# A kernel of two transformer blocks: the FFN row factor moves from its input to Silu and product, three last down units go by token tile, and the next stage's first rows are turned in the last unit

## What is computed

```python
def rmsnorm(x, g):
    y = xf * lax.rsqrt(jnp.mean(xf * xf, axis=-1, keepdims=True) + EPS)
    return y.astype(x.dtype) * g

def swiglu(x, w_gate, w_up, w_down):
    return (jax.nn.silu(x @ w_gate) * (x @ w_up)) @ w_down

h = h + 0.5 * rmsnorm(swiglu(rmsnorm(h, ffn1_pre_g), gate, up, down), ffn1_post_g)   # FFN1
h = h + rmsnorm(merged @ w_out, mix_post_g)                                          # mixer's output
h = h + 0.5 * rmsnorm(swiglu(rmsnorm(h, ffn2_pre_g), ...), ffn2_post_g)              # FFN2
x = x + y @ w_out_2                                                                  # second block's output
x = x + swiglu(rmsnorm(x, ffn_norm_g_2), ...)                                        # FFN3
```

## Time and profile before

| | |
|---|---|
| median of 3 runs | 1169.39 us (1167.99 to 1169.9) |
| profiled execution | 1170.61 us |
| its span | 1168.8 us |
| TensorE busy | 1123.3 us (96%) |
| TensorE weight loads | 942.0 us (81%) |
| VectorE busy | 694.4 us (59%) |
| ScalarE busy | 586.1 us (50%) |
| mean granted TensorE clock | 0.990 of full speed |

### The profile page before, as it was taken

The page is one execution under the profiler, slowest core; times in us unless marked ns, Lnnn a source line. Parts: engine busy times, 40 slices in busy tenths (PEclk is TensorE's granted clock), DMA queues, the critical chain, the costliest instruction groups (busy, mean ns, idle before and its releaser), DMA issues. The chain is left out here.

```text
span 1168.8 us, 13926 instructions
## 1 busy us (share of the span) xinstructions
PE 1123.3 (96%) x5748; PEld 942.0 (81%) x5748; DVE 694.4 (59%) x793; ACT 586.1 (50%) x828; POOL 21.4 (2%) x35
## 2 busy tenths in 40 slices
PE   5999999999999999999999999999899999999997
PEld 4888887899989986777778888877778877888886
DVE  4644554676767777776666445446665656555443
ACT  4543434554567765664455434345566535343333
POOL 0000000000001110000000000000000000000000
PEclk9999999899999999999999999999999999999999
DMA  9656653655566544445456565554633345566550
GB/s 306 213 180 189 195 193 115 218 179 180 176 188 199 185 154 167 143 123 184 146 185 210 183 195 195 183 152 140 203 109 126 131 139 182 181 191 197 187 180 36
DMA packets 132206, 202.74 MB, mean 173 GB/s; under 512 B 5760, under 2 KB 98816, under 8 KB 131888
## 3 DMA queue, kind: packets, MB, share of 16 engines
q1 hardware_dynamic: 129328, 190.68, 50.6%
q0 software_dynamic: 2816, 11.18, 2.8%
HBM read 200.76 MB, written 1.08 MB: 173 GB/s over the span
## 5 line engine op out<-in xcount | busy, mean ns | idle before, releaser
L913 DVE TENSOR_TENSOR WL<-RAW,WH 128x2048 fp32r<-128x2048 f32 (+1 forms) x181 | 406.2, 2265 | 111.1 <-ACT WH L437 111.1
L437 ACT ACTIVATE WH<-RAW 128x2048 fp32r<-128x2048 f32 (+1 forms) x181 | 338.5, 1888 | 12.6 <-DMA RAW<-in_w_out 3.7
L1479 PE MATMUL PS<-WH,XTH 128*128 128x512 f32 (+1 forms) x676 | 267.3, 395 | 0.0
L1481 PE MATMUL PS<-WH,XTL 128*128 128x512 f32 (+1 forms) x676 | 263.4, 390 | 0.0
L1480 PE MATMUL PS<-WL,XTH 128*128 128x512 f32 (+1 forms) x676 | 262.8, 389 | 0.0
L1479 PE MATMUL ACC<-WH,KTH 128*128 128x512 f32 (+1 forms) x476 | 188.7, 396 | 5.7 <-DVE WL L913 3.5
L1481 PE MATMUL ACC<-WH,KTL 128*128 128x512 f32 (+1 forms) x476 | 185.8, 390 | 0.0
L1480 PE MATMUL ACC<-WL,KTH 128*128 128x512 f32 (+1 forms) x476 | 185.4, 390 | 0.0
L1481 PEld LDWEIGHTS PS<-WH,XTL 128*128 128x128 f32 x676 | 126.8, 188 | 26.5
L1479 PEld LDWEIGHTS PS<-WH,XTH 128*128 128x128 f32 x676 | 127.0, 188 | 24.9 <-issue 0.5
L1480 PEld LDWEIGHTS PS<-WL,XTH 128*128 128x128 f32 x676 | 127.1, 188 | 24.6
(11 more groups left out here) (264 smaller groups left out, 1283.0 us busy)
## 6 DMA issues: line engine op xcount, KB each, us to landing
RAW<-in_w_in SPq DMA_DIRECT2D x50, 1024.0 KB, 5.2
RAW<-in_ffn_w_gate SPq DMA_DIRECT2D x44, 512.0 KB, 4.0
RAW<-in_ffn_w_up SPq DMA_DIRECT2D x44, 512.0 KB, 5.0
RAW<-in_ffn_w_down SPq DMA_DIRECT2D x22, 1024.0 KB, 4.9
RAW<-in_w_gate SPq DMA_DIRECT2D x22, 512.0 KB, 4.0
RAW<-in_w_up SPq DMA_DIRECT2D x22, 512.0 KB, 5.0
RAW<-in_w_down SPq DMA_DIRECT2D x11, 1024.0 KB, 4.9
RAW<-in_ssd_w_branch SPq DMA_DIRECT2D x8, 1024.0 KB, 5.0
```

The costliest lines, as they stand in the source:

```text
L437: nc.scalar.activation(WH[:, s, 0:n], RAW[:, s, 0:n], ACT.Copy).then_inc(w_hi, 1)
L913: tt(WL[:, s, 0:n], RAW[:, s, 0:n], WH[:, s, 0:n].bitcast(F32), ALU.subtract).then_inc(w_lo, 1)
L1479: mm(ps, stat_hi, mov_hi, start=first, stop=False)
L1481: return mm(ps, stat_lo, mov_hi, start=False, stop=last)
```

## The change

1. The input of an FFN (n = 0, 2, 4) is XN = H * gain, without the row factor. The factor comes in behind the product: as the scale of Silu and as a scalar of the product for HS. So XN waits for H alone, and the Silus wait for the factor. The squares for these factors write to a scratch JUNK, no longer to XN. ScalarE computes them after the copy XTH of tile 0 (n = 2, 4) or of both tiles (n = 0).
2. The last three down units of an FFN go by token tile: 8, 9, 10 for tile 0, then for tile 1, the turn of the last hidden rows behind unit 8 of tile 0. Those last hidden rows go to LASTH and LASTL, places in XTH and XTL, since KTH and KTL still hold the two steps before. In step 10 two weight splits move from behind the Silus to in front of them.
3. The next stage's tile 0 is turned (`first_tile`) inside the last unit: before the last 6 matmuls of FFN1 and FFN2, and before the last 12 of the second block's output product. For n = 2 it stays behind the last unit.

The core of the diff:

```diff
+        JUNK = SCR[:, 0:1024]
+        LASTH, LASTL = (x[:, 0:4, P:2 * P] for x in (XTH, XTL))
...
+                junk = JUNK if n in (0, 2, 4) else XN[:, t, :]
+                own.link(nc.scalar.activation(junk, H[:, t, :], ACT.Square, accum_out=SS[:, t:t + 1]))
...
-                    if 0 < j < FF_STEPS - 1:
+                    if j:
                         split_hi()
                         split_hi()
                     c = u0 + FF_AT["a", j]
                     for t in range(NT):
                         chunk_tile(c, c + 1, t)
-                        nc.scalar.activation(SG[:, t, :], PS[4 + t][:, 0:256], ACT.Silu).then_inc(gate_ok, 1)
+                        act.wait_ge(rstd_ok, 4 * f + t + 1)
+                        nc.scalar.activation(SG[:, t, :], PS[4 + t][:, 0:256], ACT.Silu,
+                                             scale=RS[:, t:t + 1]).then_inc(gate_ok, 1)
                     if 1 <= j < FF_STEPS - 2:
                         split_hi()
-                    if j in (0, FF_STEPS - 1):
+                    if j == 0:
                         split_hi()
                         split_hi()
...
+                if m in (1, 3):
+                    if m == 1:
+                        y_rstd(m, unit, 0, half)
+                        y_rstd(m, unit, 1, half)
+                    xn_hi(m + 1, 0)
+                    h_rstd(m + 1, 0)
+                    h_rstd(m + 1, 1)
+                    nc.scalar.preload_act_table(next_table)
+                    xn_hi(m + 1, 1)
+                    split_hi()
+                    return
...
             ln_exp()
-            h_rstd(0, 0)
             xn_hi(0, 0)
             split_hi()
+            split_hi()
+            xn_hi(0, 1)
+            h_rstd(0, 0)
             h_rstd(0, 1)
-            split_hi()
             nc.scalar.preload_act_table(ACT.Silu)
-            xn_hi(0, 1)
             split_hi()
             ffn(0, U_FFN1)
...
             def xn(n, t):
-                dve.wait_ge(rstd_ok, NT * n + t + 1)
+                if n in (1, 3):
+                    dve.wait_ge(rstd_ok, NT * n + t + 1)
+                elif n == 0:
+                    dve.wait_ge(x_loaded[t], 16)
+                else:
+                    dve.wait_ge(h_done, NT * (n - 1) + t + 1)
                 dve.wait_ge(gpre_loaded, 16 * (n + 1))
                 for q in range(2):
                     a = slice(q * 512, (q + 1) * 512)
-                    stt(XN[:, t, a], H[:, t, a], RS[:, t:t + 1], GPRE[:, a], ALU.mult, ALU.mult).then_inc(xn_ok, 1)
+                    if n in (1, 3):
+                        ins = stt(XN[:, t, a], H[:, t, a], RS[:, t:t + 1], GPRE[:, a], ALU.mult, ALU.mult)
+                    else:
+                        ins = tt(XN[:, t, a], H[:, t, a], GPRE[:, a], ALU.mult)
+                    ins.then_inc(xn_ok, 1)
...
-                        tt(HS[:, t, :], PS[4 + t][:, 256:512], SG[:, t, :], ALU.mult).then_inc(h_ready, 1)
+                        stt(HS[:, t, :], PS[4 + t][:, 256:512], RS[:, t:t + 1], SG[:, t, :], ALU.mult,
+                            ALU.mult).then_inc(h_ready, 1)
...
+            def first_tile(n):
+                turn_normed(n, 0, 0)
+                turn_normed(n, 0, 1)
...
-                down(FF_STEPS - 3)
-                turn_hidden(FF_STEPS - 1)
-                pe.wait_ge(hT_lo, n0 + FF_STEPS - 1)
-                pe.wait_ge(w_lo, u0 + FF_AT["d", FF_STEPS - 2] + 1)
-                s = FF_STEPS - 2
+                s = FF_STEPS - 3
                 for t in range(NT):
-                    for n in range(2):
+                    for n in range(3):
                         c = u0 + FF_AT["d", s + n]
+                        if t == 0 and n == 1:
+                            turn_hidden(FF_STEPS - 1)
                         pe.wait_ge(w_lo, c + 1)
                         pe.wait_ge(hT_lo, n0 + s + n + 1)
-                        ins = rows_part(c, [(0, t), (1, t)], False, n == 1, half=(s + n) % 2)
+                        half_at = 2 if n == 2 else (s + n) % 2
+                        rows_part(c, [(0, t)], False, n == 2, half=half_at)
+                        if t and n == 2 and then:
+                            then()
+                        ins = rows_part(c, [(1, t)], False, n == 2, half=half_at)
...
+            first_tile(0)
             norm(0, U_FFN1)
-            ffn(0, U_FFN1)
+            ffn(0, U_FFN1, then=lambda: first_tile(1))
             norm(1, U_XZ)
...
+            first_tile(2)
             norm(2, U_FFN2)
-            ffn(1, U_FFN2)
+            ffn(1, U_FFN2, then=lambda: first_tile(3))
...
-            by_pairs(20, U_OUT2, BUF2, ready=lambda s: pe.wait_ge(merged, 4 + (1, 3, 2, 4)[s]), turned=True)
+            by_pairs(20, U_OUT2, BUF2, ready=lambda s: pe.wait_ge(merged, 4 + (1, 3, 2, 4)[s]), turned=True, then=lambda: first_tile(4))
             norm(4, U_FFN3)
             ffn(2, U_FFN3)
```

More of the change, by code:

```diff
@@ L456, in h_rstd @@
                 own.wait() if own.n else None
-                own.link(nc.scalar.activation(XN[:, t, :], H[:, t, :], ACT.Square, accum_out=SS[:, t:t + 1]))
+                junk = JUNK if n in (0, 2, 4) else XN[:, t, :]
+                own.link(nc.scalar.activation(junk, H[:, t, :], ACT.Square, accum_out=SS[:, t:t + 1]))
                 own.link(nc.scalar.activation(RS[:, t:t + 1], SS[:, t:t + 1], ACT.Ln, scale=1.0 / D, bias=EPS))
@@ L476, in hidden_hi @@
                     act.wait_ge(h_turned, n0 + j + 1)
-                    nc.scalar.activation(KTH[:, half_of(j)], PS[6][:], ACT.Copy).then_inc(hT_hi, 1)
+                    if j == FF_STEPS - 1:
+                        nc.scalar.activation(LASTH, PS[6][:].rearrange("p (k c) -> p k c", k=4), ACT.Copy).then_inc(hT_hi, 1)
+                    else:
+                        nc.scalar.activation(KTH[:, half_of(j)], PS[6][:], ACT.Copy).then_inc(hT_hi, 1)
                 for j in range(FF_STEPS):
@@ L517, in boundary @@
                     return
-                if m in post_no:
-                    y_rstd(m, unit, 1, half)
+                y_rstd(m, unit, 1, half)
                 xn_hi(m + 1, 0)
                 h_rstd(m + 1, 1)
-                if next_table:
-                    nc.scalar.preload_act_table(next_table)
                 xn_hi(m + 1, 1)
@@ L934, in hidden_lo @@
                     dve.wait_ge(hT_hi, n0 + j + 1)
-                    tt(KTL[:, half_of(j)], PS[6][:], KTH[:, half_of(j)].bitcast(F32), ALU.subtract).then_inc(hT_lo, 1)
+                    if j == FF_STEPS - 1:
+                        tt(LASTL, PS[6][:].rearrange("p (k c) -> p k c", k=4), LASTH.bitcast(F32),
+                           ALU.subtract).then_inc(hT_lo, 1)
+                    else:
+                        tt(KTL[:, half_of(j)], PS[6][:], KTH[:, half_of(j)].bitcast(F32), ALU.subtract).then_inc(hT_lo, 1)
                 for j in range(FF_STEPS):
@@ L1408, in _, with turn_normed @@
             mm = nc.tensor.matmul
-            def norm(n, c):
-                def turn(t, q):
-                    pe.wait_ge(xn_ok, 4 * n + 2 * t + q + 1)
-                    if t:
-                        pe.wait_ge(xt_lo, 4 * n + q + 1)
-                    for k in range(4):
-                        j = 4 * q + k
-                        ins = nc.tensor.transpose(PS[6 + q][:, k * P:(k + 1) * P], XN[:, t, j * P:(j + 1) * P], IDENT)
-                    ins.then_inc(xn_turned, 1)
-                turn(0, 0)
-                turn(0, 1)
+            def turn_normed(n, t, q):
+                pe.wait_ge(xn_ok, 4 * n + 2 * t + q + 1)
+                if t:
+                    pe.wait_ge(xt_lo, 4 * n + q + 1)
+                for k in range(4):
+                    j = 4 * q + k
+                    ins = nc.tensor.transpose(PS[6 + q][:, k * P:(k + 1) * P], XN[:, t, j * P:(j + 1) * P], IDENT)
+                ins.then_inc(xn_turned, 1)
+            def first_tile(n):
+                turn_normed(n, 0, 0)
+                turn_normed(n, 0, 1)
+            def norm(n, c):
                 pe.wait_ge(w_lo, c + 1)
@@ L1433, in norm @@
                 half(c + 1, 1, 0, 4, (0, 1))
-                turn(1, 0)
+                turn_normed(n, 1, 0)
                 half(c + 1, 1, 0, 4, (2, 3)).then_inc(chunk_half, 1)
-                turn(1, 1)
+                turn_normed(n, 1, 1)
                 pe.wait_ge(xt_lo, 4 * n + 3)
@@ L1509, in rows_part @@
                     a = slice(half * 512 + k * TOK + t * P, half * 512 + k * TOK + (t + 1) * P)
+                    hi, lo = (LASTH[:, 2 * k + t], LASTL[:, 2 * k + t]) if half == 2 else (KTH[:, a], KTL[:, a])
                     for h in range(2):
                         ws = slice(k * D + h * 512, k * D + (h + 1) * 512)
-                        ins = parts(PS[banks + 2 * t + h][:], KTH[:, a], KTL[:, a], WH[:, s, ws], WL[:, s, ws],
+                        ins = parts(PS[banks + 2 * t + h][:], hi, lo, WH[:, s, ws], WL[:, s, ws],
                                     first and k == 0, last and k == 1)
```

(2 more changed lines are left out.)

2 lines of the change are left out of this document (1 added, 1 removed).

## The result

The changed kernel takes **1176.47 us** in the median of 5 runs (1173.48 to 1178.73). The kernel before, timed between those runs, takes 1169.40 (5 runs). The ratio is 1.0058 with a 95% interval of 1.0038 to 1.0078, so the change costs between 4.4 and 9.1 us. The forecast was 1174.4 in a range of 1172.0 to 1178.0: the sign and the range hold, and the forecast's +5.0 lies in the measured interval, in its lower part.

A forecast was written before the change was run, and what follows sets the result against it. TensorE, busy nearly all the span, bounds the kernel; only added work or its waits count. 4.5 + 1.3 - 0.9 - 0.8 + 0.9 = +5.0 us on the median 1169.39 gives 1174.4, range 1172.0 to 1178.0.

The forecast's parts named there:

- Start, +4.5: Start of FFN1: factors and table load ahead of unit 2's split delay TensorE's step 1 by 4.5 us.
- Clock at the start, +1.3: Behind the start's wait: a certain fall to the lower clock, priced 0.5 to 2.3 us, value 1.3.
- FFN ends, -0.9: FFN1 and FFN2 ends: hidden-row wait goes, but squares still precede the copy; 0.45 us gained per joint, -0.9 together.
- Mixer's joint, -0.8: Joint after the mixer's output product: squares no longer held by the factor, first matmul at 599.7 against 600.33; -0.8 us.
- Second block's joint, +0.9: Joint after second block's output product: turn inside the unit waits 1.6 us for the late add; +0.9 us.
- The rule on transposes: Second block's joint: transposes don't count as busy for the clock gate, so it may lose 1.6 us more.
- Small edits, 0: Three-operand HS products, Silu scales from a row and a later freed unit: 0, or 0.1 us in step 1.
- The clock at the other joints: Joints other than the start: six stretches without a 128x512 matmul before and after, so 0 us, 1.6 each for the range.
- The first: Rival: two more joints fall to 1.2 GHz, or one and a longer start stretch; 1177.6 us, chance 0.20.
- The second: Rival: start's delay mostly hidden, or joints give their whole idle; 1168.6 to 1171.0 us, chance 0.10.
- third: Rival: ScalarE's order doesn't end these waits, so unit 2 and XTH copies aren't late; 1164.5 us, chance 0.04.

The follow-up runs named there:

- e1: Changed kernel with both row factors and the Silu table load put back before the tile 1 copies at the start; 1171.23 us, ratio 1.0015.
- e8: Changed kernel with 18 matmuls that nothing reads in TensorE's wait at the start, ahead of step 1 of FFN1; 1174.88 us, ratio 1.0050.
- e2: Changed kernel with XTH copied before the squares of tile 1's sum and XTL before VectorE's gain at the two FFN joints; 1174.38 us, ratio 1.0031.
- e3: Changed kernel with FFN3's first tile turned behind the second block's output product, not inside its last unit; 1174.88 us, ratio 1.0040.
- e4: Changed kernel with the next stage's first tile turned behind the last down unit of FFN1 and FFN2, not inside it; 1173.47 us, ratio 1.0035.
- e7b: Changed kernel with the start's order put back and nine matmuls that nothing reads in the wait at both FFN joints; 1168.77 us, ratio 0.9995.
- e5: Kernel before with only the three last down units by token tile, with their hidden copies and split order; 1169.19 us, ratio 0.9998.
- e6: Changed kernel with the start's order and all three first-tile turns put back, keeping the missing factor and down units by tile; 1166.42 us, ratio 0.9966.
- e12: Kernel before with only the down units by token tile, run again for a second profile; profiled execution 1165.21 us.
- e9: Kernel before with the three last down units by tile, plus five matmuls that nothing reads at both FFN joints; 1168.67 us, ratio 0.9984.

## Why the prediction was right, step by step

- **Start, +4.5.** Right. Unit 2 was split at 29.97 (forecast 29.6; the first matmuls ran longer at the lower clock in this execution, and the two factors began at 25.53 instead of 25.11), and TensorE waited 4.46 us. e1 takes the step away and gets 0.43 points of 0.58 back.
- **Clock at the start, +1.3.** Right in mechanism, as e8 shows, and too small in size: 1.6 in the changed kernel's trace, but 2.4 in those of e2, e3 and e4, above the 2.3 that I had as its upper end. I had priced one slow stretch of the usual length with a part of it inside the wait. In the changed kernel's trace it began only with the matmuls, so nothing was hidden; in the other three it did begin in the wait, but was twice as long (3.4 us lost by the windows, 2.4 of it in matmuls).
- **FFN ends, -0.9.** Right in mechanism and size. The KTL wait is gone, the two turns came in (0.93 where I had 0.87), the copy stayed behind the squares. The account gives -0.5 for FFN2 (-0.21 and -0.28); FFN1's can't be separated from the start within a few tenths. e4 and e2 show the two halves of the reason: the turn inside the unit costs 0.93 and gains nothing, and what ends the joint is the chain of tile 1.
- **Mixer's joint, -0.8.** Right: last matmul to first 2.64 instead of 3.40. The table's other 1.3 is the missing slow stretch.
- **Second block's joint, +0.9.** Right to a tenth in the chain: from the add's start to the turn 2.12 us (forecast 2.1), to the first matmul 5.98 (forecast 5.9), to the low matmuls 8.12 (forecast 8.1); the account has +2.65 - 1.82 = +0.8. The true wait was 1.31, not 1.6. Here the term held two effects of opposite sign that the prediction didn't part: e3 shows some 1.5 us lost by the turn's place against 0.7 won by the missing factor.
- **The rule on transposes.** No slow stretch followed this joint in the profiled run: the matmuls from 977.73 on stand 0.23 apart. Nor did one in e1, e2, e4, e7b and e8, which turn in the output unit too. The Trainium skill (TensorE: Matmul & The Clock Gate, Part 4: PE-mode transpose) says that transposes don't count as busy for the clock gate in the way matmuls do. Six traces without a fall speak rather against taking this stretch for idle as a whole, but they don't refute the page: waits with no transpose in them had no fall behind them either in many executions, as the 1.88 at 581 and the 2.25 at both FFN joints of this same trace.
- **Small edits, 0.** Right. The product for HS went from 421 to 482 ns, the Silu from 384 to 474, and no wait shows either.
- **The clock at the other joints, "0 on balance".** This is the other term that was mis-sized. I counted stretches without a 128x512 matmul and took six of them as equal to six before. They weren't: at the FFN joints that count took the transposes for idle time, and the true idle time went from 1.07 us in two pieces to 2.25 in one. In e1 both fell, and filling them gave 0.20 points or about 2 us. The five runs' median lies 2.1 above the forecast. That clock is behind it is likely: the median execution had 0.990 against 0.993 in the profiled one, 3.5 us more of full clock lost. A start of 2.4 instead of 1.3 gives 1.1 of the 2.1, and this term can give the rest; how much each gives can't be told, as the ratio's interval is 4.7 us wide and the changed kernel's own profiled run has no fall at its FFN joints, nor have those of e3 and e8, whose joints are the same. The count also left out the longest wait behind the start in the trace of before, and a fall did follow it (the window 846 to 848 has 0.54):

```profile
845.26 0.49 PE L1852 MATMUL PS<-GAIN 64*128 64x128 f32 x2 [3.08 <-DVE SM L1350]
```

- **Rivals.** The first (more slow stretches, 1177.6) came nearer than the forecast: the median lies 1.1 below it and 2.1 above the forecast. So the sign, the delay at the start and the joints' terms were foreseen, but that the time stayed inside the range owes something to luck with the clock. The second and third are ruled out by the wait of 4.46 us and by unit 2's split at 29.97, later than 25.6.

## What to carry to other kernels

Ask of each wait which chain it hangs on before moving what stands beside it: a turn put ahead of the wait saves only if the copy behind it can go at once, and if not, it takes TensorE's time from where there was idle time to spend. On an in-order engine, work that filled an idle gap costs its whole duration once it is moved behind the event that ended the gap (4.5 us for two factors and a table load). And count what a wait does to the clock apart from its length: a wait of 2.25 us that was followed by the lower clock cost 1.2 more here, and useless matmuls in it were free.

## What the runs showed of the hardware

- The same wait is followed by the lower clock in some executions and not in others. Counted over the 14 profiled executions, by TensorE's true idle time (a fall counts that begins in the wait or within 2 us behind it; "after" is the changed kernel):

```
idle time, us    place                              waits   followed by a fall
1.13             mixer's joint, factor missing        8       0
1.34             ends at 333 to 344 us               14       0
1.38             FFN joints of e4, e5, e6, e12        8       0
1.5 to 1.6       ends at 947 to 958 us               14       0
1.57             mixer's joint, old order             4       2
1.31 to 1.88     turn in the output unit              6       0
1.88             [rows 6]                            13       7
1.93 to 1.94     ends at 826 to 838 us               14       8
2.19 to 2.21     turn of tile 1 in e2                 2       0
2.25             FFN joints of after, e1, e3, e8      8       2 (both e1)
3.07 to 3.11     ends at 839 to 851 us               14      11
4.44 to 4.46     start of after, e2, e3, e4           4       4
```

  Behind the 1.88 us a fall costs 1.6 to 1.7 us; behind the start's 4.4 us it cost 1.6 or 2.4. Within one kernel these stretches are most of the spread: the quickest and the slowest of e9's 12 executions lie 8.5 us apart, and their granted clocks (0.996 and 0.989) make 8.2 of it.
- The clock falls without any idle time too, among the 128x32 matmuls behind 220 us. It did so in the profiled execution of every kernel here, for 1.7 to 5.1 us lost.
- At the start the clock rises at different moments: the turn of tile 1, behind the same 18 matmuls, came 6.83 us after the first matmul in the changed kernel's trace, 6.16 in that of before and 5.77 in that of e8.
- An execution of e5 takes either some 1165.4 us or 1168.8 and more, with nothing between in 13. The granted clock accounts for five of the slower ten; for the five at 1168.8 to 1169.3 the cause stays open.
